# A fused attention and gMLP layer on eight cores: a second set of activation buffers, the gate's product on VectorE, and a reordered end

## What is computed

```python
def reference(x, norm_g, w_in, b_in, attn_sinks, sgu_ln_g, sgu_ln_b, sgu_w, sgu_b,
              w_out, b_out, final_norm_g):
        h = rmsnorm(x, norm_g[l])
        proj = jnp.einsum('bsd,de->bse', h, w_in[l]) + b_in[l]      # (B,S,IN_WIDTH)
        q, k, v, z_a, u_s, v_s, z_s = jnp.split(proj, split_points, axis=-1)
        # sliding window of 128, 8 query heads, 2 key heads, one sink per head
        attn = banded_sink_attention(q, k, v, attn_sinks[l]) * jax.nn.silu(z_a)
        u_s = jax.nn.gelu(u_s, approximate=False)
        v_s = jax.nn.gelu(v_s, approximate=False)
        # u * (W_s LN(v) + b), W_s lower triangular 128 x 128 per group of 64 channels
        sgu = chunked_spatial_gating(u_s, v_s, sgu_w[l], sgu_b[l], sgu_ln_g[l], sgu_ln_b[l]) * jax.nn.silu(z_s)
        mixed = jnp.concatenate([attn, sgu], axis=-1)                 # (B,S,MIX_WIDTH)
        x = x + jnp.einsum('bse,ed->bsd', mixed, w_out[l]) + b_out[l]
    return rmsnorm(x, final_norm_g)
```

## Time and profile before

| what | value |
|---|---|
| median of 3 runs | 545.64 us (543.52 to 546.6) |
| profiled execution | 545.42 us |
| its span on core 7, the slowest | 543.9 us |
| spans of the 8 cores | 535.9 to 543.9 us |
| TensorE busy, in matmuls | 508.9 us, 94% |
| ScalarE, VectorE, GpSimd busy | 362.0, 351.4, 213.0 us |

### The profile page before, as it was taken

The page is one execution under the profiler, slowest core; times in us unless marked ns, Lnnn a source line. Parts: engine busy times, 40 slices in busy tenths (PEclk is TensorE's granted clock), DMA queues, the critical chain, the costliest instruction groups (busy, mean ns, idle before and its releaser), DMA issues.

```text
span 543.9 us, 9873 instructions; the slowest of 8 cores (535.9 to 543.9 us)
## 1 busy us (share of the span) xinstructions
PE 508.9 (94%) x3090; PEld 236.8 (44%) x3090; DVE 351.4 (65%) x583; ACT 362.0 (67%) x693; POOL 213.0 (39%) x302
## 2 busy tenths in 40 slices
PE   8897796999999999999999999998999999999891
PEld 3465343445344544444344444444444545434230
DVE  1946896287564677567755777557665737586764
ACT  4479945466867665776667667677657766887861
POOL 2002746136443444337244344335434442235440
PEclk9998987999999999999999999999999999999897
DMA  7999959549325710475013830365105830010112
GB/s 218 320 344 309 189 85 210 130 154 219 55 79 138 215 34 2 149 187 130 1 40 131 241 55 1 118 174 153 23 4 155 240 68 2 1 40 39 40 77 116
DMA packets 20067, 66.48 MB, mean 122 GB/s; under 512 B 2992, under 2 KB 3376, under 8 KB 20016
## 3 DMA queue, kind: packets, MB, share of 16 engines
q1 hardware_dynamic: 13680, 46.87, 23.8%
q0 software_dynamic: 5760, 18.88, 20.4%
q10 hardware_dynamic: 576, 0.11, 0.1%
HBM read 51.17 MB, written 16.78 MB: 125 GB/s over the span
## 4 chain that ended last, share of the span: by engine, by line
PE 67%; DMA 10%; DVE 7%; ACT 6%; issue 5%; POOL 3%; POOLq 0%; DVEq 0%; ACTq 0%; SPq 0%
PE pb L450 36%; PE pb L650 14%; DMA x_t<-x 7%; DMA zaT<-w_in 3%; PE pb L582 3%; PE pb L484 3%; PE pb L547 3%; PE pb L514 3%; PE pb L436 2%; ACT xn_bf L404 2%; DVE y_t L658 2%; PE pb L623 2%; PE pb L586 1%; PE pb L423 1%; DVE w_in_bf L376 1%
## 5 line engine op out<-in xcount | busy, mean ns | idle before, releaser
L450 PE MATMUL pb<-xT,w_in_bf 128*128 128x512 bf16 x1088 | 251.4, 384 | 8.6 <-DVE w_in_bf L376 4.4
L450 PEld LDWEIGHTS pb<-xT,w_in_bf 128*128 128x128 bf16 x1088 | 103.2, 99 | 140.5 <-issue 27.9
L650 PE MATMUL pb<-w_out_bf,mixT 128*128 128x512 bf16 x448 | 101.0, 379 | 0.4 <-DVE st_mv L499 0.4
L555 ACT ACTIVATE PT<-pb 128x512 bf16<-128x512 f32 x126 | 65.3, 599 | 24.2 <-PE pb L547 23.4
L601 POOL TENSOR_TENSOR LR<-LR,zaT 128x512 f32<-128x512 f32 x32 | 40.5, 1264 | 87.1 <-ACT LR L599 87.1
L560 POOL TENSOR_SCALAR_AFFINE_SELECT PT<-PT 128x512 bf16<-128x512 bf16 x62 | 45.1, 800 | 60.5 <-ACT PT L555 60.5
L650 PEld LDWEIGHTS pb<-w_out_bf,mixT 128*128 128x128 bf16 x448 | 43.0, 98 | 53.5 <-issue 3.7
L595 ACT ACTIVATE LR<-pb,esink_col 128x128 f32<-128x128 f32 x128 | 36.7, 381 | 28.2 <-PE pb L586 28.2
L389 ACT ACTIVATE xn_bf<-x_t 128x1024 bf16<-128x1024 f32 x32 | 33.6, 1049 | 24.6 <-DMA x_t<-x 24.2
L514 PE MATMUL pb<-w_in_bf,xT 128*128 128x512 bf16 x224 | 49.8, 379 | 0.0
L658 DVE TENSOR_TENSOR y_t<-pb,x_t 128x512 f32<-128x512 f32 x64 | 41.1, 684 | 12.0 <-PE pb L650 12.0
(11 more groups left out here) (74 smaller groups left out, 603.6 us busy)
## 6 DMA issues: line engine op xcount, KB each, us to landing
x_t<-x SPq DMA_DIRECT2D x32, 512.0 KB, 6.4
x_t<-bout_bc POOLq DMA_DIRECT2D x32, 512.0 KB, 6.9
out<-y_t SPq DMA_DIRECT2D x32, 512.0 KB, 2.9
x_t<-w_in SPq DMA_DIRECT2D x4, 512.0 KB, 12.8
y_t<-w_in SPq DMA_DIRECT2D x4, 512.0 KB, 16.9
mixT<-w_in SPq DMA_DIRECT2D x4, 512.0 KB, 16.9
w_out_bf<-w_out POOLq DMA_DIRECT2D x8, 256.0 KB, 9.5
sgt<-w_in SPq DMA_DIRECT2D x2, 512.0 KB, 17.8
```

The costliest lines, as they stand in the source:

```text
L450: ins = e.matmul(pbank[b.i][:], lhsT=w_in[:, k, col:col + 128], rhs=xT[:, st % 2, k, :], start=(k == 0), stop=(k == 7))
L555: S.op("act", lambda e, b=b, pt=pt: e.activation(out=pt, in_=pbank[b.i][:], func=AF.Exp, scale=0.125), reads=[b], writes=[("PT", pp, kb, g ...
L650: ins = e.matmul(pbank[banks[hf].i][:], lhsT=mx[:, ec, tt * 128:(tt + 1) * 128], rhs=w_out[:, ec, hf * 512:(hf + 1) * 512], start=(ec == 0 ...
```

## The change

**Buffers of x.** The slots are split: tiles 8 and up are loaded twice. For the norm they go through slots 0 to 2 (`NXN = 3`), loaded in `norm_stats`; for the residual sum they are loaded again into slots 3 to 7 after `project(n)` (tile n + 5), with the bias transfer right behind. 24 more loads of 512 KB result. The norm's statistics are recorded one tile at a time. From tile 27 on the result is made in place in `x_t`.

**Engines.** u times Silu(z_s) (L644 of the changed kernel) is on VectorE. The scaling of supertile 1 is on VectorE too.

**Start.** Tiles 4 to 7 are queued after weight group 11, the gating constants ahead of the last four groups; the engines that scale the weights rotate (ScalarE takes the first). 32 zero matmuls in place of 46.

**End.** The last supertile's units are recorded in another order: z_a, then attention between vs, u and z_s, then the gating. The last tile is finished in halves, and its second half is stored through ScalarE's queue.

**Planner.** The allowance between engines is 130, TensorE's window 8; issue costs and the port flag of GpSimd's transfers are changed. The program has 54 small activations that stand for a table change, 33 before.

```diff
-CONV_ENG = ["dve", "dve", "act"] * 8
+CONV_ENG = ["act", "dve", "dve"] * 8
-    PE_WINDOW = 10
-    HOP = 90.0
+    PE_WINDOW = 8
+    HOP = 130.0
...
+        def norm_slot(n):
+            return n if n < NX else (n - NX) % NXN
+
+        def sum_slot(n):
+            return n if n < NX else NXN + (n - NX) % (NX - NXN)
...
+                slot = norm_slot(4 * st + tt)
+                if st > 1:
+                    load_x(4 * st + tt, slot)
...
-            if st == 0:
+            if st < 2:
                 S.op("dve", lambda e: e.tensor_scalar(out=xn[:, tt, :], in0=xs, scalar1=st_rs[:, tt:tt + 1], scalar2=None, op0=ALU.mult),
...
-                S.op("pool", lambda e, jj=jj: e.tensor_tensor(out=gate[:, jj, :], in0=uT[:, jj, :], in1=zsT[:, jj, :], op=ALU.mult),
+                on_dve = True
+                S.op("dve" if on_dve else "pool",
+                     lambda e, jj=jj: e.tensor_tensor(out=gate[:, jj, :], in0=uT[:, jj, :], in1=zsT[:, jj, :], op=ALU.mult),
...
+            halves = [(0, 1)] if n < NT - 1 else [(0,), (1,)]
...
-            if n + NX < NT:
-                load_x(n + NX)
+            if NXN <= n < NT - NX + NXN:
+                load_x(n + NX - NXN, slot)
+                add_bout(n + NX - NXN)
...
-        for tt, count in ((0, 24), (1, 8), (2, 8), (3, 6)):
+        for tt, count in ((0, 20), (1, 4), (2, 4), (3, 4)):
...
+        last_st = NS - 1
+        n = 4 * last_st
+        for c in range(4):
+            za_unit(last_st, c)
         scores(n)
+        for tt in range(4):
+            vs_unit(last_st, tt)
         scores(n + 1)
-        project(n - 2)
         values(n)
+        for c in range(4):
+            u_unit(last_st, c)
         scores(n + 2)
         values(n + 1)
-        project(n - 1)
+        for c in range(4):
+            zs_unit(last_st, c)
         scores(n + 3)
         values(n + 2)
-        project(n)
+        mixing(last_st)
+        project(n - 2)
         values(n + 3)
-        for tt in range(1, 4):
+        project(n - 1)
+        for tt in range(4):
             project(n + tt)
```

More of the change, by code:

```diff
@@ L21 @@
 NX = 8
+NXN = 3
 NBANK = 8
@@ L437, in mm @@
                 return ins
-            S.op("pe", mm, reads=["ones64", "US"], writes=[b], t=216 * count)
+            S.op("pe", mm, reads=["ones64", "US"], writes=[b], t=290 * count)
         def xT_keys(st):
@@ L636, in mixing @@
                 S.op("dve", lambda e, jj=jj, sg=sg: e.tensor_tensor(out=mx[:, 4 + jj, :], in0=sgt[:, sg, :], in1=gate[:, jj, :], op=ALU.mult),
-                     reads=[("sgt", sg), ("gate", jj)], writes=[("mixS" + mk, jj)] + ([("xT", NS % 2, tt) for tt in range(4)] if mk else []), t=650, port=True)
+                     reads=[("sgt", sg), ("gate", jj)], writes=[("mixS" + mk, jj)], t=650, port=True).deps.update(held_by(mk))
         def project(n):
@@ L653, in project @@
-            S.op("pe", mmo, reads=[("mixA" + mk, tt)] + [("mixS" + mk, jj) for jj in range(4)] + [("w_out", k) for k in range(8)], writes=banks, t=3460)
-            def resid(e):
-                ins = None
-                for hf in range(2):
-                    ins = e.tensor_tensor(out=y_t[:, ys, hf * 512:(hf + 1) * 512], in0=pbank[banks[hf].i][:],
-                                          in1=x_t[:, slot, hf * 512:(hf + 1) * 512], op=ALU.add)
-                return ins
-            S.op("dve", resid, reads=banks + [("x", slot)], writes=[("y", ys)], t=1280)
@@ L662, in project, with half, mmo @@
-            if n + NX < NT:
-                load_x(n + NX)
-            S.op("act", lambda e: e.activation(out=xn[:, 3, :], in_=y_t[:, ys, :], func=AF.Square, accum_out=st_fs[:, ys:ys + 1]),
-                 reads=[("y", ys)], writes=[("xn", 3), ("fs", ys)], t=1230)
+            halves = [(0, 1)] if n < NT - 1 else [(0,), (1,)]
+            def half(v, hf):
+                return v[:, hf[0] * 512:(hf[-1] + 1) * 512]
+            for hs in halves:
+                def mmo(e, hs=hs):
+                    ins = None
+                    for hf in hs:
+                        for ec in range(8):
+                            ins = e.matmul(pbank[banks[hf].i][:], lhsT=mx[:, ec, tt * 128:(tt + 1) * 128],
+                                           rhs=w_out[:, ec, hf * 512:(hf + 1) * 512], start=(ec == 0), stop=(ec == 7))
+                    return ins
+                S.op("pe", mmo, reads=[("mixA" + mk, tt)] + [("mixS" + mk, jj) for jj in range(4)] + [("w_out", k) for k in range(8)],
+                     writes=[banks[hf] for hf in hs], t=1730 * len(hs))
@@ new lines, in project, with resid @@
+            for hs in halves:
+                def resid(e, hs=hs):
+                    ins = None
+                    for hf in hs:
+                        ins = e.tensor_tensor(out=half(y, (hf,)), in0=pbank[banks[hf].i][:], in1=x_t[:, slot, hf * 512:(hf + 1) * 512], op=ALU.add)
+                    return ins
+                S.op("dve", resid, reads=[banks[hf] for hf in hs] + [("x", slot)],
+                     writes=[yk if len(hs) > 1 else yk + hs], t=640 * len(hs))
+                if len(hs) == 1:
+                    S.op("act", lambda e, hs=hs: e.activation(out=half(xn[:, sq, :], hs), in_=half(y, hs), func=AF.Square,
+                                                              accum_out=st_hs[:, hs[0]:hs[0] + 1]),
+                         reads=[yk + hs, yk], writes=[("xn", sq, hs), ("hs", hs)], t=750)
@@ new lines, in project @@
+            if NXN <= n < NT - NX + NXN:
+                load_x(n + NX - NXN, slot)
+                add_bout(n + NX - NXN)
+            if len(halves) == 1:
+                S.op("act", lambda e: e.activation(out=xn[:, sq, :], in_=y, func=AF.Square, accum_out=st_fs[:, ys:ys + 1]),
+                     reads=[yk], writes=[("xn", sq), ("fs", ys)], t=1230)
+            else:
+                S.op("dve", lambda e: e.tensor_tensor(out=st_fs[:, ys:ys + 1], in0=st_hs[:, 0:1], in1=st_hs[:, 1:2], op=ALU.add),
+                     reads=[("hs", hs) for hs in halves], writes=[("fs", ys)], t=150)
@@ L780, in build_program @@
         values(3)
-        add_bout(0)
+        for n in range(4):
+            add_bout(n)
         v_unit(1)
@@ L791, in build_program @@
         rest(1)
-        for st in range(1, NS):
+        for st in range(1, NS - 1):
             n = 4 * st
             nx = st + 1
-            more = nx < NS
-            if not more:
-                break
+            final = nx == NS - 1
             scores(n)
@@ L840, in build_program @@
         with nc.Block() as block:
-            S.emit(block, [S.lw[("out", n)] for n in range(NT)])
+            S.emit(block, [o for k, o in S.lw.items() if isinstance(k, tuple) and k[0] == "out"])
     return nc
```

120 lines of the change are left out of this document (68 added, 52 removed).

## The result

The changed kernel takes 532.31 us (median), the kernel before 545.46 on the same chip. The ratio is 0.9754, with an interval of 0.9713 to 0.9795: 13.1 us less. The forecast was 535.0, between 526.5 and 543.0. Where one run of a kernel was in the chip's slower state (here the fourth, 619.01), the median counts it and the ratio, formed from the other runs, does not, so the ratio decides. The profiled execution took 530.92, its span is 529.4 on core 1, the slowest.

What follows compares the result with a forecast made beforehand. The prediction took TensorE as the bound, busy for 508.9 of 543.9 us. Its terms, 9.5 + 3.2 - 5.6 + 3.7 = 10.8 us saved, gave a span of 533.1 and a forecast of 535.0, range 526.5 to 543.0.

Steps and rivals of the forecast that it cites:

- Start: From the first weight groups to project(3): TensorE's waits and slow matmuls shrink, 9.5 us saved, between 5 and 13.
- The two waits that it struck out: TensorE's start waits of 2.30 us for the last weight conversion and 4.29 for US, both counted as gone.
- the new losses: At the start: VectorE is full between 48 and 75 us, so WT and mixing's banks come late, 2.5 us.
- The two causes: At the start: GpSimd's gate products slowing the weight conversion, and its bias transfers issued ahead of its mask.
- Middle: Between start and end: waits for scaled x go, new table changes cost some; 3.2 us saved, between -4 and 5.
- End: Last supertile: TensorE idles about 6.1 us for mixing, then slows; net 5.6 us lost, between 2 and 9.
- the four shorter waits: Last supertile, before the long wait: banks freed late by ScalarE's table change, Exp and Ln; 0.8, 0.7, 0.9, 0.4 us.
- After the last matmul: Final sums, norm and store, last tile in halves: 7.3 us instead of 11.0, 3.7 saved.
- Rival 2: ScalarE decides: new table changes fall between scores and values; 555 us if all 21 are exposed; chance 0.08.
- Rival 3: VectorE and GpSimd exclude each other more, at start, end and some supertiles: 10 us, 544 to 545; chance 0.10.
- Rival 4: Early norm of x brings nothing because transfers are late anyway: 540 us; chance 0.10 including mixtures up to 543.
- Rival 1: Smaller gap at the end and start nearly free of stalls: 18.5 us saved, 527; chance 0.17.

Runs made afterwards that it cites:

- e2: The changed kernel with 46 zero matmuls as before in place of 32: 533.62 us, ratio 0.9766 to the kernel before.
- e5: The kernel before with only the gate products moved from GpSimd to VectorE: 543.59 us, ratio 0.9967.
- e6: The kernel before with only GpSimd's first eight bias transfers moved behind its masks of the fourth scores: 545.37 us, ratio 0.9994.
- e10: The kernel before with gate products on VectorE and the first eight bias transfers placed as in the changed kernel: 540.8 us, ratio 0.9898.
- e1: The changed kernel with the last supertile's gating recorded earlier, remaining attention among the projections, planned anew: 529.45 us, ratio 0.969 to the kernel before.
- e3: The changed kernel with the last tile finished in one piece: 534.64 us, ratio 0.9786 to the kernel before.
- e8: The changed kernel with Exp in place of Gelu and Silu, one table load instead of 54: 532.34 us, ratio 0.9765 to the kernel before.
- e4: The changed kernel with the 32 gate products back on GpSimd, orders otherwise kept: 536.3 us, ratio 0.9818 to the kernel before.
- e7: The kernel before with Exp in place of Gelu and Silu, one table load instead of 33: 558.74 us, ratio 1.0234.
- e9: The kernel before with Exp in place of Gelu and Silu and the gate products on VectorE: 543.72 us, ratio 0.9951.
- e11: The changed kernel with one slot per tile of x, loaded once, planned anew: 544.16 us, ratio 0.9976 to the kernel before.

## Why the prediction was right, and where its sizes were off

- **Start.** 9.5 saved was said, between 5 and 13; it is 12.2 (124.8 to 112.6; on core 7, as in the rows of before, 11). The two waits that it struck out are gone, and the masks stand ahead of six transfers as said. The mis-sized term is the new losses, put at 2.5: TensorE waits 0.28 for an `xT` and 0.73 for a bank of mixing, 1.0; no wait for `WT` is left. The clock before the first group costs 1.43 (1.85 said), and e2 shows that even this is hidden. The two causes were counted as separate sums; e5, e6 and e10 show that they bring less singly than together (1.8 and 0 against 5.6 in the whole time, 2.6 and 1.5 against 5.8 at `project(3)`).
- **Middle.** 3.2 saved was said; the spans leave 3.0 (from 112.6 to the end of the last matmul, 522.4, it is 409.8, before 408.1; 1.7 lost, and the end alone lost 4.7). This sets core 1 against core 7. Core by core this stretch, the end's 4.7 included, is 0.3 us longer on core 7 and 1.0 on core 5, which had waited 4.9 and 4.8 for the scaled x, and 5.0 longer on core 3, which had waited 0.2: some 4 us gained on the slow cores, nothing on the quick one. So the term is right because the metric is the slowest core. Waits for L416 are 1.2 in all, where under 1 was the sign named, and one of 0.94 for `xT` stands behind them; for Exp it is 0.8. ScalarE's busy time, 389 said, is 387.1. That the second set of buffers is what removed the wait is argued: no run shows it alone.
- **VectorE.** 371 us was said, 348.0 is measured. The step that failed is that nothing else on VectorE was to get shorter, and with it the price of 531 ns for a product of 128x512, taken from the mask: that mean had the waits for GpSimd in it. The price is 5 of the 23 us, masks, `vln` and weight conversions are 4 to 5 each. The product takes 420, and with GpSimd's products gone the masks fell to 468 and `vln` to 543 (in e5, where that is all that changed, from 531 to 494 and from 679 to 553):

```profile
L575 DVE TENSOR_TENSOR PT<-PT,mask_sb 128x512 bf16<-128x512 bf16 x64 | 27.8, 468 | 8.1 <-ACT PT L566 7.6
L515 DVE TENSOR_SCALAR vln<-vs_f,st_mv,st_lr 128x512 bf16<-128x512 f32 x32 | 17.3, 543 | 6.9 <-POOL st_lr L513 6.4
L644 DVE TENSOR_TENSOR gate<-uT,zsT 128x512 bf16<-128x512 bf16 x32 | 12.4, 420 | 7.2 <-ACT zsT L468 7.2
```

- **End.** The wait of 6.1 is 4.69, the slow matmuls 2.3 (1.9 said), the four shorter waits 0.41, 0.84, 1.00 and 0.63 (0.8, 0.7, 0.9, 0.4 said). Together 9.9 for 10.8, net 4.7 lost for 5.6. The wait is shorter because VectorE had done part of its list beside `values(31)`: two mixing steps and a sum lie before 501.45, the end of the values. e1 shows the cause.
- **After the last matmul.** 7.0 (7.3 said), from 11.0; e3 prices the halves at 1.0.
- **The sum.** 12.2 + 3.0 - 4.7 + 4.0 = 14.5, the difference of the spans (the middle is what the others leave, so this is no check of it). The forecast had 10.8; most of what it lacks is the start.
- **The rivals.** Rival 2 (tables) is refuted by e8. Rival 3 (VectorE and GpSimd exclude each other more) had the mechanism right and the sign wrong: taking the products off GpSimd removes the exclusion. That move is worth 1.8 us in the kernel before (e5) and 2.7 in the changed one (e4), and 15 where the products fall beside the layer norm (e7 against e9). Rival 4 (the early norm brings nothing) stays open: e11 is slower by 12 us, but not by waits for the scaled x. The planner's new constants (window, allowance) were not tested alone either. Rival 1, 527, was near in the start (12.2 of 13) but not in the end; e1 comes within 2.5 of it by mending that.
